# First stage of a transformer block on one Trainium2 core: two pairs of channels from the un-normalised input, one sum product, channels 2 and 3 in banks of their own

## Chip, cores and metric

One core of one Trainium2 chip (trn2) runs the whole program. The metric is device time in microseconds (us) of one execution. The kernel before took 2967.39 us as the median of 3 runs (2961.52, 2967.39 and 2967.43).

## The reference

The input x has 512 tokens of 1024 features. A first block adds attention and a gated linear recurrence to x, and then a layer of 128 x 128 experts; a second block adds a feed-forward layer, a mixer and a second feed-forward layer. The change touches only the recurrence at the very start of the first block:

```python
h = rms_norm(x, norm1_g)          # x * rsqrt(mean(x*x) + eps) * gain
z = h @ w_in
q, k, v, xr, yr, gate_logits = jnp.split(z, IN_SPLITS, axis=-1)
rnn = rg_lru(causal_depthwise_conv(xr, conv_w, conv_b), ...) * gelu(yr)
merged = gates[:, :, 0] * (attn @ w_br_attn) + gates[:, :, 1] * (rnn @ w_br_rnn)
```

xr and yr have 1280 columns each, ten blocks of 128, which the kernel calls channels c = 0 to 9. The root mean square of a token is a factor per token, so it may be put on x before the product with w_in or on the product after it. The convolution has four taps over the tokens. rg_lru takes two sigmoid gates from small products of the convolved channel (w_rg), forms a decay and an input, and scans over the tokens.

## The kernel before

Features lie on the 128 partitions and tokens along the free dimension, so X is 8 tiles (k = 0 to 7) of 128 x 512. Everything is computed in fp32 by a split: each operand is a high part (rounded to fp32r) and a low part (the rest), and a product of two 128-blocks is three matmuls, high x high, high x low and low x high (triple, L718 to L721). A weight unit of 128 output columns is 8 blocks, hence 24 matmuls of 512 columns (linear, L723). A weight unit is loaded by SP into one of 5 raw buffers (load, L2454), copied by ACT to its high part (split on ACT, L1281, recorded at L1279), and its low part is taken on DVE (split on DVE, L1760, recorded at L1750). Five pairs of high and low parts exist (NW = 5); the high part of unit j may be written when the product of unit j - 5 is done. The order of the units is written out by hand (unit_order). It begins with w_in 24, 34, 25, 35 (units 0 to 3: xr and yr of channels 0 and 1), then 26, 36, 27, 37 (units 4 to 7, channels 2 and 3), two units of gate columns (8, 9), two small w_rg units (10, 11), four units of channels 4 and 5 (12 to 15), and so on; the group of channels 8 and 9 has no gate columns, and the units after it are four of w_br_rnn (34 to 37, 640 columns) and two of w_rg (38, 39).

Each engine runs its own program in order, and they meet only at semaphores. The names that matter:

- SP: recurrence (L2481) issues the parameters, the four quarters of x, the constants cst, units 0 to 4, the lambdas and units 5 and 6. load waits before unit j until the low part of unit j - 5 is taken.
- ACT: recurrence (L1353) squares each tile of X into scr (L1276) and forms the high part of x times gain, gh (L1358). Then norm (L1305): the root from the sum (Ln and Exp in root, L1292) goes to scr[8], and eight high parts of the normalised H are copied. Then per channel d: the copy of the xr bank to pad (called xr_raw), the high part of the convolved channel (conv_hi), and the Gelu of the yr bank (gelu). Each change of function set on ACT is an ACT_TABLE_LOAD.
- DVE: gained (L1770) forms the low part of x times gain; norm (L1775) scales X into scr (L1758) and takes the low part of H (L1750). conv4 (L1815) is the convolution of one channel, four instructions and the low part of its result; for channel 0 it first scales xr and yr by the root. scalars (L1788) is a chain of some 35 tiny instructions for lambda and the softplus, with two Exp on ACT in it, and stands after channel 1. rnn_gates (L1832) is the DVE side of the gates and the scan.
- TensorE (PE): recurrence (L789) waits for cst, multiplies a matrix of ones with the 8 squares into bank 7 (sums, L754), then runs channel 0 from x times gain, the two units side by side (two, L733), so that it need not wait for the root. Channels 1 to 9 are products with the normalised H. After each pair from the second on: two gate units of the pair (gates_of_rnn, L762, called rgate) into banks 4 and 6, and the four small products of the pair before (rnn_products, L772, called br and bx) into banks 4 to 7.

PSUM has eight banks of 512 columns. xr of channel d goes to bank d % 2 and yr to bank 2 + d % 2, so channel d waits until channel d - 2 has been read. The product br of channel c waits for the sigmoid of the gate unit c (rgate) that read the same bank:

```python
q.wait_ge(dve, ("conv_parts", c))
if c < 6:
    q.wait_ge(act, ("rgate", c))
```

## Time and profile before

| | |
|---|---|
| median of 3 runs | 2967.39 us |
| the profiled execution | 2965.4 us |
| its span, first to last instruction | 2963.3 us |
| PE (matmul) busy | 2910.5 us, 98% |
| DVE, ACT, POOL busy | 64%, 39%, 28% |
| mean granted TensorE clock | 0.996 |

Times in rows are us from the start of the span. A row of a timeline is: start, duration, engine, line and operation, output<-inputs, shape and count, and in brackets the idle time of the engine before it and what ended it. Rows of matmuls overlap: a row's duration holds its way through the array, and the distance between two starts is what one costs in a stream. The 2.1 us between the span and the profiled execution's time lie outside the instructions. A granted clock of 1.00 is 2.4 GHz and 0.50 is 1.2 GHz.

### The profile page before, as it was taken

To read this page: it belongs to the slowest core of one execution; us is meant where nothing else is said; L and a number is where in the kernel's file an instruction comes from. 1 tells how busy PE (TensorE), PEld (TensorE's weight loads), DVE (VectorE), ACT (ScalarE), POOL (GpSimd) and SP (SyncE) were. 2 spreads that over 40 slices of the span, in tenths; PEclk is the share of its full clock that TensorE was granted. 3 is DMA by queue.
4 is the path that set the end of the run, shared out by engine and by line. 5 is a ranking of instruction groups with operands and counts; after the bars stand their busy time and mean duration, and the time that the engine had idled before them with its cause. 6 is when DMAs were issued, how large, how long until landed. Compare 5 with 4: busy or idle time off the path is not lost.

```text
span 2963.3 us, 35559 instructions
## 1 busy us (share of the span) xinstructions
PE 2910.5 (98%) x13947; PEld 2495.4 (84%) x13947; DVE 1909.2 (64%) x3257; ACT 1151.8 (39%) x1704; POOL 842.5 (28%) x521
## 2 busy tenths in 40 slices
PE   8999999999999999999999999999999999899999
PEld 6877777789889999998999999998888877688887
DVE  6664666578888895426878788865434577644443
ACT  5674565443333334433233223323222256632221
POOL 0000000128788888882332233321000300210000
PEclk9999999999999999999999999999999999999999
DMA  4325564436656676799988899842232321133222
GB/s 140 114 90 214 199 224 166 133 103 138 139 122 139 153 159 141 173 250 321 339 308 309 287 319 322 298 160 98 92 102 93 111 92 50 50 100 100 92 93 71
DMA packets 240807, 489.28 MB, mean 165 GB/s; under 512 B 97664, under 2 KB 149440, under 8 KB 240128
## 3 DMA queue, kind: packets, MB, share of 16 engines
q1 hardware_dynamic: 175680, 417.87, 43.0%
q0 software_dynamic: 64960, 69.14, 10.2%
q8 instruction: 110, 1.80, 0.2%
q14 instruction: 57, 0.47, 0.0%
HBM read 443.18 MB, written 77.23 MB: 176 GB/s over the span
## 4 chain that ended last, share of the span: by engine, by line
PE 80%; DVE 12%; ACT 4%; POOL 2%; issue 2%; DMA 1%; SPq 0%; POOLq 0%
PE pb L719 25%; PE pb L721 25%; PE pb L720 25%; DVE whl L1750 2%; POOL gd L2408 2%; ACT scr L1276 1%; DVE ST L1758 1%; DVE S L1750 1%; ACT whl L1279 1%; DVE su L1999 1%; DVE ST L2000 1%; DVE scr L1750 1%; DVE su L2002 1%; PE pb L1014 1%; DVE ST L1750 1%
## 5 line engine op out<-in xcount | busy, mean ns | idle before, releaser
L719 PE MATMUL pb<-H,whl 128*128 128x512 f32 (+1 forms) x2400 | 940.0, 392 | 6.4 <-DVE whl L1750 2.3
L721 PE MATMUL pb<-H,whl 128*128 128x512 f32 (+1 forms) x2400 | 911.8, 380 | 0.0
L720 PE MATMUL pb<-H,whl 128*128 128x512 f32 (+1 forms) x2400 | 911.2, 380 | 0.0
L1750 DVE TENSOR_TENSOR whl<-raw,whl 128x1024 fp32r<-128x1024 f32 (+5 forms) x554 | 652.5, 1192 | 252.7 <-ACT whl L1279 251.4
L1279 ACT ACTIVATE whl<-raw 128x1024 fp32r<-128x1024 f32 (+5 forms) x554 | 544.6, 1003 | 356.4 <-PE pb L721 355.2
L719 PE MATMUL pb<-S,whl 128*128 128x448 f32 (+2 forms) x1732 | 654.0, 378 | 13.9 <-DVE S L1750 6.1
L720 PE MATMUL pb<-S,whl 128*128 128x448 f32 (+2 forms) x1732 | 649.2, 375 | 0.0
L721 PE MATMUL pb<-S,whl 128*128 128x448 f32 (+2 forms) x1732 | 648.8, 375 | 0.0
L719 PEld LDWEIGHTS pb<-H,whl 128*128 128x128 f32 x2400 | 451.4, 188 | 84.0 <-issue 9.5
L720 PEld LDWEIGHTS pb<-H,whl 128*128 128x128 f32 x2400 | 451.4, 188 | 72.9 <-issue 6.0
L721 PEld LDWEIGHTS pb<-H,whl 128*128 128x128 f32 x2400 | 450.6, 188 | 72.3
L2408 POOL DMA_INDIRECT gd<-scr,place x256 | 438.5, 1713 | 137.7 <-issue 76.2
L719 PEld LDWEIGHTS pb<-S,whl 128*128 128x128 f32 x1732 | 327.0, 189 | 60.3 <-DVE S L1750 7.6
L720 PEld LDWEIGHTS pb<-S,whl 128*128 128x128 f32 x1732 | 327.2, 189 | 42.4 <-issue 1.0
L721 PEld LDWEIGHTS pb<-S,whl 128*128 128x128 f32 x1732 | 327.1, 189 | 42.4
L2387 POOL TENSOR_TENSOR pad<-X 128x512 f32<-128x512 f32 x31 | 43.5, 1404 | 856.5 <-DVE X L1750 828.8
L1276 ACT ACTIVATE scr<-pb 128x448 f32<-128x448 f32 (+1 forms) x130 | 70.9, 546 | 383.8 <-PE pb L721 359.8
L1750 DVE TENSOR_TENSOR scr<-pb,scr 128x512 f32<-128x512 f32 x96 | 66.0, 690 | 210.7 <-PE pb L721 199.7
L2441 POOL DMA_INDIRECT scr<-in_pv_rows,su x64 | 94.9, 1483 | 232.1 <-DVE scr L1758 204.8
L1279 ACT ACTIVATE S<-GA 128x896 fp32r<-128x896 f32 x60 | 57.2, 953 | 253.5 <-DVE GA L1750 253.5
L2395 POOL DMA_INDIRECT scr<-in_pu_rows,su x64 | 92.1, 1440 | 215.1 <-DVE scr L1758 166.4
L1750 DVE TENSOR_TENSOR X<-X,pb 128x448 f32<-128x448 f32 (+1 forms) x144 | 86.1, 628 | 91.0 <-PE pb L721 75.9
(226 smaller groups left out, 2516.7 us busy)
## 6 DMA issues: line engine op xcount, KB each, us to landing
raw<-in_pu SPq DMA_DIRECT2D x128, 512.0 KB, 4.4
raw<-in_pv SPq DMA_DIRECT2D x128, 512.0 KB, 6.2
raw<-in_w_in SPq DMA_DIRECT2D x72, 512.0 KB, 3.7
ad<-scr SPq DMA_DIRECT2D x128, 224.0 KB, 4.5
GA<-gd SPq DMA_DIRECT2D x60, 448.0 KB, 4.2
GA<-ad SPq DMA_DIRECT2D x60, 448.0 KB, 5.5
raw<-in_wg SPq DMA_DIRECT2D x44, 512.0 KB, 3.7
raw<-in_wu SPq DMA_DIRECT2D x44, 512.0 KB, 4.2
```

Source lines behind the costliest of these rows:

```text
L719: e.matmul(o, lh, h, start=start, stop=False, skip_group_check=True)
L720: e.matmul(o, lh, l, start=False, stop=False, skip_group_check=True)
L721: return e.matmul(o, ll, h, start=False, stop=stop, skip_group_check=True)
L1014: last = e.matmul(bank[gbank[n % 4]][:, c], hot2[n % 4][:, c], hot1[n % 4][:, c], start=True, stop=True, skip_group_check=True)
L1276: return e.activation(o, x, func, **kw)
L1279: return e.activation(o, x, ACT.Copy)
L1750: return e.tensor_tensor(o, x, y, op)
L1758: return e.scalar_tensor_tensor(out=o, in0=x, scalar=s, in1=y, op0=op0, op1=op1, **kw)
L2387: e.tensor_tensor(one_sq if k else sum_sq, x, x, ALU.mult).then_inc(pool.up(), 1)
L2395: e.indirect_dma_start(urow[j % 3] if j < UROWS else tail_row[j % 4], None, a["pu_rows"], bass.IndirectOffsetOnAxis(ap=expert[:, j:j + 1], ...
L2408: e.indirect_dma_start(g_rows, bass.IndirectOffsetOnAxis(ap=place[:, b, h, k:k + 1], axis=0), TSv[:, b, h, k:k + 1], None, compute_op=ALU. ...
L2441: e.indirect_dma_start(tail_row[j % 4], None, a["pv_rows"], bass.IndirectOffsetOnAxis(ap=expert[:, j:j + 1], axis=0)).then_inc(row_in[j % ...
```

## The change

TensorE. The 8 products for the sum of squares become one, of a tile scr[0] in which DVE has added the squares; it is issued after the first block (k = 0) of channel 1, and the wait for cst goes with it. Channels 0 and 1 both come from x times gain, by two. Channels 2 and 3 get banks 4 and 5 (xr) and 6 and 7 (yr) instead of 0 to 3. The banks 4 to 7 are those of the gate units and the small products, so the first of these now wait for the reads of channels 2 and 3 (xr_raw and gelu).

```diff
+        def x_bank(d):
+            return bank[(4 if d in (2, 3) else 0) + d % 2]
+        def y_bank(d):
+            return bank[(6 if d in (2, 3) else 2) + d % 2]
...
+        g1h, g1l = cut(S_t[:, 1024:5120], 8), cut(S_t[:, 6144:10240], 8)
...
-            def two(j, outs, hh, hl, ready, done, tag=None):
+            def two(j, outs, hh, hl, ready, done, tag=None, at_k=4):
...
-                    if k == 4 and tag:
+                    if k == at_k and tag:
...
             def sum_of(tag):
-                if tag == "4":
+                if tag == "1":
+                    q.wait_ge(cst_in, "cst")
+                    q.wait_ge(dve, "sq_sum")
+                elif tag == "4":
...
-                e.matmul(bank[7], ones, sum_sq, start=True, stop=True, skip_group_check=True).then_inc(
+                e.matmul(bank[7], ones, scr[0] if tag == "1" else sum_sq, start=True, stop=True, skip_group_check=True).then_inc(
...
-            def sums(tag, sq, b, lhs=ones):
-                for k, s in enumerate(sq):
-                    q.wait_ge(act, ("sq", tag, k))
-                    last = e.matmul(b, lhs, s, start=k == 0, stop=k == len(sq) - 1, skip_group_check=True)
-                last.then_inc(prod.up(("sums", tag)), 1)
...
             def gates_of_rnn(m):
...
-                q.wait_ge(act, ("r_sig", m - 2) if m > 1 else 0)
+                q.wait_ge(act, ("r_sig", m - 2) if m > 1 else ("gelu", 2) if m else ("xr_raw", 2))
...
             def rnn_products(pair):
...
+                    if c < 2:
+                        q.wait_ge(act, ("gelu", 3) if c else ("xr_raw", 3))
...
             def recurrence():
-                q.wait_ge(cst_in, "cst")
-                sums("1", scr[0:8], bank[7])
+                g1 = [("g", "1", k) for k in range(8)]
...
-                        if d == 0:
-                            j = q.unit("w_in", 24)
-                            q.unit("w_in", 34)
-                            two(j, (bank[0], bank[2]), gh, gl, [("g", "1", k) for k in range(8)], (("xr", 0), ("yr", 0)))
+                        if d < 2:
+                            j = q.unit("w_in", 24 + d)
+                            q.unit("w_in", 34 + d)
+                            two(j, (bank[i], bank[2 + i]), g1h, g1l, g1, (("xr", d), ("yr", d)), "1" if d else None, 1)
...
-                        if d == 2:
-                            q.wait_ge(dve, "xr_scaled")
-                        elif d > 2:
+                        if d in (4, 5):
+                            q.wait_ge(dve, ("xr_scaled", d - 4))
+                        elif d > 5:
...
-                        linear(q.unit("w_in", 24 + d), bank[i], Hh, Hl, h1, ("xr", d))
-                        if d > 1:
+                        linear(q.unit("w_in", 24 + d), x_bank(d), Hh, Hl, h1, ("xr", d))
+                        if d in (4, 5):
+                            q.wait_ge(dve, ("yr_scaled", d - 4))
+                        elif d > 5:
...
-                        linear(q.unit("w_in", 34 + d), bank[2 + i], Hh, Hl, h1, ("yr", d))
+                        linear(q.unit("w_in", 34 + d), y_bank(d), Hh, Hl, h1, ("yr", d))
...
```

ACT. A set of functions is loaded at the start, and the loads before the first Square and the first Ln are not asked for. The high parts of weights are mixed in among the squares, and in the loop over channels the high parts of up to three more units are made, at the head of each channel. Channel 1 has no copy to pad any more.

```diff
         def scalar(eng, e):
-            q, hi_done, logs = Waits(eng, units), [0], [False]
+            q, hi_done, logs = Waits(eng, units), [0], [True]
+            e.preload_act_table_set("natural_log_exp_and_others")
...
-            def norm(tag, sq, r, b, hi, mid=lambda: None, free=()):
+            def norm(tag, sq, r, b, hi, mid=lambda: None, free=(), between=lambda k: None):
...
+                    between(k)
...
             def recurrence():
...
-                for k in range(8):
-                    q.wait_ge(x_in[k // 2], ("x", k // 2))
-                    run(ACT.Square, scr[k], X[k]).then_inc(act.up(("sq", "1", k)), 1)
-                    e.activation(gh[k], X[k], ACT.Copy, scale=prm("norm1_g", k)).then_inc(act.up(("ghi", "1", k)), 1)
+                for k in range(10):
+                    if k < 8:
+                        q.wait_ge(x_in[k // 2], ("x", k // 2))
+                        e.activation(g1h[k], X[k], ACT.Copy, scale=prm("norm1_g", k)).then_inc(act.up(("ghi", "1", k)), 1)
+                    if k == 1:
+                        split(2)
+                    elif k > 1:
+                        run(ACT.Square, scr[k - 2], X[k - 2]).then_inc(act.up(("sq", "1", k - 2)), 1)
...
-                        split(2)
-                norm("1", scr, scr[8], bank[7], Hh, lambda: split(4))
+                        split(3)
+                    elif k == 7:
+                        split(4)
+                norm("1", scr, scr[8], bank[7], Hh, lambda: split(5), between=lambda k: split(6) if k == 5 else None)
...
-                        weights("w_in", 24 + d)
-                        if d == 0:
-                            weights("w_in", 34)
-                        if d:
+                        split(q.unit("w_in", 24 + d) + NW + 2)
+                        q.unit("w_in", 34 + d)
+                        if d > 1:
...
-                            q.wait_ge(dve, ("conv", d - 2) if d > 1 else ("pad0", i))
-                            copy(pad[i][:, 32:544], bank[i]).then_inc(act.up(("xr_raw", d)), 1)
+                            q.wait_ge(dve, ("conv", d - 2))
+                            copy(pad[i][:, 32:544], x_bank(d)).then_inc(act.up(("xr_raw", d)), 1)
...
-                        if d:
-                            weights("w_in", 34 + d)
...
-                        if d:
+                        if d > 1:
...
-                            q.wait_ge(dve, "yr_scaled")
-                        run(ACT.Gelu_apprx_tanh, rlf[d], bank[2 + i] if d else rlf[0]).then_inc(act.up(("gelu", d)), 1)
+                            q.wait_ge(dve, ("yr_scaled", d))
+                        run(ACT.Gelu_apprx_tanh, rlf[d], y_bank(d) if d > 1 else rlf[d]).then_inc(act.up(("gelu", d)), 1)
...
```

DVE. It adds the squares, takes low parts of weights inside norm, scales xr of channel 0 inside norm, and scales xr and yr of channel 1 as well as of channel 0 in conv4. In the loop the low parts of up to three more units are taken at the head of each channel.

```diff
-            def norm(tag, xs, gains, sq, r, hi, lo, mid=lambda: None):
+            def norm(tag, xs, gains, sq, r, hi, lo, mid=lambda: None, between=lambda k: None):
...
+                    between(k)
...
+            def scaled_x(c):
+                q.wait_ge(prod, ("xr", c))
+                tt(pad[c][:, 32:544], bank[c], scr[8], ALU.mult).then_inc(dve.up(("xr_scaled", c)), 1)
             def conv4(c, beside=()):
...
-                if c:
+                if c > 1:
...
-                    q.wait_ge(prod, ("xr", 0))
-                    then(tt(pad[0][:, 32:544], bank[0], scr[8], ALU.mult), "xr_scaled")
-                    q.wait_ge(prod, ("yr", 0))
-                    tt(rlf[0], bank[2], scr[8], ALU.mult).then_inc(dve.up("yr_scaled"), 1)
+                    if c:
+                        scaled_x(1)
+                    q.wait_ge(prod, ("yr", c))
+                    tt(rlf[c], bank[2 + c], scr[8], ALU.mult).then_inc(dve.up(("yr_scaled", c)), 1)
+                    q.wait_ge(dve, dve.n)
...
             def recurrence():
...
-                for k in range(8):
-                    gained("1", k, "norm1_g", gh, gl, ("g", "1", k))
-                    if k == 5:
+                for k in range(10):
+                    if k < 8:
+                        gained("1", k, "norm1_g", g1h, g1l, ("g", "1", k))
+                    if k == 1:
...
+                    elif k == 8:
+                        split(4)
+                    if k > 2:
+                        q.wait_ge(act, ("sq", "1", k - 2))
+                        then(tt(scr[0], scr[0], scr[k - 2], ALU.add), *(["sq_sum"] if k == 9 else []))
+                norm("1", X, gains("norm1_g"), scr, scr[8], Hh, Hl, between=lambda k: scaled_x(0) if k == 2 else split(5) if k == 4 else split(6) if k == 7 else None)
...
-                norm("1", X, gains("norm1_g"), scr, scr[8], Hh, Hl, lambda: split(4))
...
-                        weights("w_in", 24 + d)
-                        if d == 0:
-                            weights("w_in", 34)
+                        split(q.unit("w_in", 24 + d) + NW + 2)
+                        q.unit("w_in", 34 + d)
...
-                        if d:
-                            weights("w_in", 34 + d)
...
```

SP. Units 0 and 1 are loaded behind the first quarter of x, ahead of the other three.

```diff
-            def load_x(name):
-                for i in range(4):
+            def load_x(name, quarters=range(4)):
+                for i in quarters:
...
             def recurrence():
...
-                load_x("x")
+                load_x("x", (0,))
+                load(2)
+                load_x("x", (1, 2, 3))
...
+                q.wait_ge(dve, ("yr_scaled", 1))
...
```

The tiles g1h and g1l that hold x times gain are moved so that the results of channels 0 and 1 do not overwrite them.

## Rows read from the trace of the kernel before

**Rows 1.** The page: span, busy time of the engines

```profile
span 2963.3 us, 35559 instructions
...
PE 2910.5 (98%) x13947; PEld 2495.4 (84%) x13947; DVE 1909.2 (64%) x3257; ACT 1151.8 (39%) x1704; POOL 842.5 (28%) x521
```

**Rows 2.** Waits of PE, first 300 us: us in total, times, longest

```profile
PE pb L757 <- DMA cst<-in_cst: 11.5, 1, 11.5
PE pb L719 <- DVE whl L1750: 5.1, 3, 2.8
PE pb L719 <- ACT scr L1276: 1.6, 1, 1.6
```

**Rows 3.** Timeline of PE, 0 to 80 us

```profile
11.50 9.68 PE L757 MATMUL pb<-scr,cst 128*128 128x512 f32 x16 [11.50 <-DMA cst<-in_cst]
...
59.98 0.47 PE L719 MATMUL pb<-H,whl 128*128 128x512 f32 x1 [0.70 <-DVE whl L1750]
...
76.61 0.39 PE L719 MATMUL pb<-S,whl 128*128 128x512 f32 x1
...
79.33 0.39 PE L719 MATMUL pb<-H,whl 128*128 128x512 f32 x1
```

**Rows 4.** Timeline of DVE, 19 to 60 us

```profile
19.01 0.29 DVE L1754 TENSOR_SCALAR prm<-prm 128x1 f32<-128x1 f32 x3
...
19.72 2.32 DVE L1750 TENSOR_TENSOR whl<-raw,whl 128x1024 fp32r<-128x1024 f32 x2
23.89 1.42 DVE L1758 SCALAR_TENSOR_TENSOR scr<-X,prm,scr 128x512 f32<-128x512 f32 x2 [1.84 <-ACT scr L1276]
...
34.67 1.23 DVE L1750 TENSOR_TENSOR whl<-raw,whl 128x1024 fp32r<-128x1024 f32 x1 [0.25 <-ACT whl L1279]
35.81 0.68 DVE L1750 TENSOR_TENSOR pad<-pb,scr 128x512 f32<-128x512 f32 x1
...
43.63 1.23 DVE L1750 TENSOR_TENSOR whl<-raw,whl 128x1024 fp32r<-128x1024 f32 x1 [2.20 <-ACT whl L1279]
...
49.32 1.22 DVE L1750 TENSOR_TENSOR whl<-raw,whl 128x1024 fp32r<-128x1024 f32 x1 [0.26 <-ACT whl L1279]
50.46 0.35 DVE L1750 TENSOR_TENSOR sm<-scr 128x64 f32<-128x64 f32 x2
...
59.75 0.54 DVE L1755 TENSOR_SCALAR ST<-pad,prm 128x512 f32<-128x512 f32 x1
```

**Rows 5.** Timeline of ACT, 0 to 113 us

```profile
5.95 1.28 ACT L1276 ACT_TABLE_LOAD   x1 [5.95 <-DMA X<-in_x]
...
40.72 1.28 ACT L1276 ACT_TABLE_LOAD   x1
42.02 0.63 ACT L1276 ACTIVATE ST<-ST 128x512 f32<-128x512 f32 x1
...
55.55 1.05 ACT L1279 ACTIVATE whl<-raw 128x1024 fp32r<-128x1024 f32 x1
...
72.85 0.69 ACT L1276 ACTIVATE scr<-pb,prm 128x512 f32<-128x512 f32 x1
...
112.17 0.69 ACT L1276 ACTIVATE scr<-pb,prm 128x512 f32<-128x512 f32 x1 [1.00 <-PE pb L721]
```

**Rows 6.** Timeline of the weight loads of PE, 11 to 17 us

```profile
15.93 0.34 PEld L757 LDWEIGHTS pb<-scr,cst 128*128 128x128 f32 x1 [0.52 <-issue]
16.73 0.19 PEld L757 LDWEIGHTS pb<-scr,cst 128*128 128x128 f32 x1 [0.46 <-issue]
```

**Rows 7.** Timeline of PE, 168 to 202 us

```profile
177.54 0.76 PE L719 MATMUL pb<-S,whl 128*128 128x512 f32 x1 [2.84 <-DVE whl L1750]
...
195.77 0.50 PE L719 MATMUL pb<-S,whl 128*128 128x512 f32 x1 [1.60 <-DVE whl L1750]
...
199.05 0.50 PE L719 MATMUL pb<-H,whl 128*128 128x512 f32 x1 [1.61 <-ACT scr L1276]
```

**Rows 8.** PE by windows of 1 us: window, busy, granted clock, DMA share, GB/s

```profile
178.00:179.00 1.00, 1.00 (x4) 0.50 0.42 122
```

## The prediction

> **What bounds the kernel now.** I read the page first: PE is busy 2910.5 of 2963.3 us [rows 1]. Only work taken from PE or its idle time can pay, and PE idles 52.8 us in all. The waits of PE over the first 300 us come next [rows 2]: 11.5 us for cst at the start, then 5.1 us for low parts of weights and 1.6 us for an ACT result. The timeline of PE places them [rows 3]: it starts at 11.50 with sixteen matmuls of the eight sum products, which take 9.68 us, and from there to 174 us it pauses once, for 0.70 us. So in this stage PE looks like the bound. The timelines of DVE and ACT must be read beside it [rows 4, 5], because the first stage is also one long chain through both: root, H, convolutions, the tiny `scalars`, Gelu, gates. Its slack behind PE is small: at 112.17 ACT waited 1.00 us for PE [rows 5], and that is all there is in a cycle of 35 us. The chain even overtakes PE at the end of the stage, where PE idles 2.84, 1.60 and 1.61 us [rows 7].
>
> What can be won is easy to count. The chain decides whether it is kept. A few terms recur: a matmul in a stream costs (79.33 - 76.61) / 12 = 0.227 us [rows 3], a unit of 24 costs 5.44, one block of one unit 0.68; a high part takes ACT 1.0 and its low part DVE 1.15 to 1.2 [rows 4, 5].
>
> **The start.** The first quarter of x has landed at 5.95 [rows 5] and cst at 11.50 [rows 3], four transfers later: 1.4 us for each. Units 0 and 1, now second and third in the queue, land at about 7.3 and 8.7, and the other quarters of x some 2.8 us later than before. The table load of 1.28 us at 5.95 moves into the time in which nothing has landed. High part, low part: PE starts at about 9.6 instead of 11.50. The clock is low at first: the weight loads of PE shrink from 0.34 to 0.19 us between 15.93 and 16.73 [rows 6], so 5.2 us ran at half speed. I take the same 5.2 us now, a loss of 2.6. Channel 0 then ends at 9.6 + 16 x 0.68 + 2.6 = 23.1, block 0 of channel 1 at 24.5, and the one sum product (0.9; 1.2 is the mean of the eight [rows 3], which includes slow ones) at 25.4. Is the sum of squares there by then? From the first high part at about 7.3 on DVE has 8 low parts of x (0.75), 4 of weights (1.2) and 7 adds (0.7, as the product of 35.81): 15.7 us, so 23.0 [rows 4]. Just in time; two more microseconds of waits for ACT would move the root by 0.6.
>
> Ln and Exp then take 1.4, with no table load between: DVE begins to scale X at 26.8. Before, it began at 23.89 [rows 4]. **The root comes 2.9 us later**, although 7 of 8 products are gone, since channel 0 now stands ahead of it. Bounds: 1.5 us to either side, by the clock and the landings.
>
> A table load in the rows costs 1.30 us: at 40.72 it begins, at 42.02 the Gelu runs [rows 5]. The Trainium skill (ScalarE: Activation LUTs, What ACT_TABLE_LOAD costs) adds a drain of about 1.38 us, 2.66 in all; by that the removed load before Ln would give back 1.4 us more, and my sum would read +3.5 instead of +4.9. The trace shows no such gap, so it decides.
>
> **What DVE does between root and channel 2.** Before, from 23.89 to the convolution of channel 2 at 59.75 [rows 4], 35.9 us. The change adds, from the same rows: low parts of units 8 and 9 (2.3) and of the small unit 10 (0.45), now at the head of channels 1 and 2; scaling of xr and yr of channel 1 (2 x 0.68); the small prm and mask instructions that stood before the root (19.01 to 19.72, 0.7). It saves 0.4: waits for high parts of 0.25, 2.20 and 0.26 us become one of 2.3 (the Gelu of channel 0 with its table load, then a high part). That is +4.4. **The convolution of channel 2 starts at 26.8 + 40.3 = 67.1, 7.3 us later than before.** `scalars`, at 50.46 before, starts at 57.3.
>
> **Where PE is meanwhile.** After the sum product: seven blocks of two units 9.5, four units 21.8, and 0.9 of waiting for the last H tiles (ready at 26.8 + 10.5 + 2.95, the three inserts in norm). It has finished channels 2 and 3, by their four banks without a wait, at 57.6. Before it was there at 59.98 + 5.5 = 65.5. **PE is 8 us ahead.** But the next is gate unit 0 in bank 4, which now waits for xr_raw of channel 2. On ACT that copy stands behind the two Exp of `scalars`, Gelu of channel 1 and high parts 9 and 10. Before, a high part stood 5.1 us after the start of `scalars` (50.46 to 55.55 [rows 4, 5]); now that point is 62.4 and the copy is done at 64.2. PE waits 6.6 us. Its two gate units take 10.9 us and some 1.7 to 3.4 more at a low clock: done at 77 to 78.5.
>
> Behind them br of channel 0 waits for the sigmoid of rgate 0, which ACT issues after channels 2 and 3: at 72.85 before [rows 5]. It inherits +7.3 from the convolution, less one high part of 1.0 and 0.3 of another that have moved ahead: 78.9, done at 79.6. br ran at 76.61 before [rows 3]. **All 8 us are spent and PE is 3.0 us late.** SP is no limit: units 5 and 6 are asked for behind the same low parts, and its new wait for yr_scaled 1 comes long after.
>
> **Channels 4 to 7.** PE was the bound and had slack 1.0 us of ACT behind it [rows 5]. The high and low parts at the head of a channel delay rgate by another 0.75 us relative to PE; under 1.0, so nothing is added and +3.0 is carried.
>
> **The end of the stage.** The units of w_br_rnn are now ready early, so the wait of 2.84 us at 177.54 goes. What is late next is the low part of unit 39 and the sigmoid of channel 8, which stand behind the gates of channels 6 and 7. For them, parts at the head of channels 8 and 9 add about 2.5 us and three of 640 columns that no longer stand later save about 2.0: +0.5. So PE waits once, some 6 us, instead of three times, and goes on at 199.05 + 3.5.
>
> **The clock.** After the 2.84 us of idle PE ran at 0.50 [rows 7, 8] for about 3 us; after 1.60 us it did not. The 6 us wait at the end costs a like stretch: 1.7 us, half of it hidden, so 0.9. The 2.0 us wait before br lies between the two rows: 0 or 1.7; I take 0.5. The rest of the program is bound by PE and shifts whole.
>
> **Sum:** 3.0 + 0.5 + 0.9 + 0.5 = +4.9 us on the profiled 2965.4, so 2970.3. That execution lies 2.0 below the median of the runs shown, 2967.39, which gives 2972. A measurement of this kernel can tell about 0.2%, 5.9 us, from no change.
>
> **The rivals.**
> Faster: the chain keeps up, or my order of it is wrong, and PE keeps its lead. For it: PE idles almost nowhere before. Against it: ACT's slack of 1.00 us and the 7.3 us counted on DVE. It needs xr_raw 2 by 57.6, 6.6 us before my estimate. Time: 2967.4 - 8.0 = 2959.4. Chance 0.12. Something halfway, 0.05.
> Slower: the clock. If the wait before br lowers it (1.7), and the long wait at the end holds it low for two such stretches, none hidden (3.4), the sum is 3.0 + 0.5 + 1.7 + 3.4 = +8.6: 2976. [...] The Trainium skill (TensorE: Matmul & The Clock Gate, Part 1) speaks for it: low is the resting state of the clock and activity lifts it. The trace agrees (0.34 then 0.19 us at the start). Chance 0.20.
> The change doesn't do what it says: the early table load doesn't hold for Ln, or units 0 and 1 land together with x. The root comes another 1.3 to 2 us late, and the sum is 6.2 to 6.9: 2974. Chance 0.08.
> My forecast has 0.55, of which 0.12 lies above the 5.9 us.
>
> **Numbers.** Faster 0.12; within 0.2%: 0.43 + 0.05 + 0.04 = 0.52; slower 0.12 + 0.20 + 0.04 = 0.36. Range: the bounds of the root (1.5), of the chain (1) and of the clock (0 to 3.4) span about +1.5 to +10; downwards it also takes in the halfway case and a run as low as the lowest shown. 2962 to 2979.
>
> **What would show it.** PE starts near 9.6; one sum product near 25; DVE scales X from 26 to 27; convolution of channel 2 near 67; PE idle 6 to 7 us for an ACT copy to pad near 64, and 2 us before the first small product at 79 to 80; no wait at 175; one of 5 to 7 us near 199, at a clock of 0.50 behind it. I am wrong if PE passes 58 to 64 us without a wait, or if the first small product starts before 76.6.

## The result and the profile after

The changed kernel takes 2972.56 us in the median of 10 runs (2967.37 to 2977.41), the kernel before 2967.23 us (10 runs, 2961.52 to 2970.21). The ratio is 1.0020, with a 95% interval of 1.0011 to 1.0029: slower by 5.3 us on the medians, just under the 5.9 us that the prediction called no change, and clear of zero. The profiled execution took 2973.16 us with a span of 2971.4. A second series of the unchanged file gave 2968.64 us (11 runs) beside 2964.47 (28 runs), ratio 1.0013 (1.0004 to 1.0022). One profile of the experiments, that of banks_undone, fell on a disturbed execution (mean clock 0.753) and is not read; the median below is of its other 11 runs.

The page and the waits of PE over the first 300 us of the kernel after:

```profile
span 2971.4 us, 35561 instructions
...
PE 2909.3 (98%) x13933; PEld 2495.9 (84%) x13933; DVE 1913.4 (64%) x3266; ACT 1150.6 (39%) x1702; POOL 842.6 (28%) x521
```

```profile
PE pb L726 <- DVE whl L1762: 15.4, 3, 9.0
PE pb L726 <- ACT pad L1287: 6.5, 1, 6.5
PE pb L726 <- ACT scr L1284: 1.9, 2, 1.6
PE pb L726 <- DVE H L1762: 0.5, 1, 0.5
```

Beside [rows 1, 2]: the first wait has shrunk from 11.5 to 9.0 us, and 6.5 us stand at a new place, a wait for ACT's copy to pad. All waits together were 18.2 us and are now 24.3. The timeline of PE, over the same stretches as [rows 3, 7]:

```profile
9.02 0.77 PE L726 MATMUL pb<-S,whl 128*128 128x512 f32 x1 [9.02 <-DVE whl L1762]
...
23.88 1.02 PE L761 MATMUL pb<-scr,cst 128*128 128x512 f32 x2
...
39.05 0.50 PE L726 MATMUL pb<-H,whl 128*128 128x512 f32 x1 [0.51 <-DVE H L1762]
...
63.57 0.80 PE L726 MATMUL pb<-H,whl 128*128 128x512 f32 x1 [6.46 <-ACT pad L1287]
...
78.86 0.47 PE L726 MATMUL pb<-S,whl 128*128 128x512 f32 x1 [1.57 <-ACT scr L1284]
...
81.70 0.39 PE L726 MATMUL pb<-H,whl 128*128 128x512 f32 x1
...
198.65 0.80 PE L726 MATMUL pb<-S,whl 128*128 128x512 f32 x1 [5.90 <-DVE whl L1762]
...
201.92 0.57 PE L726 MATMUL pb<-H,whl 128*128 128x512 f32 x1 [0.34 <-ACT scr L1284]
```

PE is through with channels 2 and 3 at 63.57 - 6.46 = 57.1, where it was at 65.5 before: 8.4 us ahead. It then gives all of that back. The first small product comes at 78.86 against 76.61, gate unit 6 at the end of the stage at 201.92 against 199.05. DVE and ACT, over the stretches of [rows 4, 5]:

```profile
26.39 1.42 DVE L1770 SCALAR_TENSOR_TENSOR scr<-X,prm,scr 128x512 f32<-128x512 f32 x2 [3.70 <-ACT scr L1284]
...
48.74 2.36 DVE L1762 TENSOR_TENSOR whl<-raw,whl 128x1024 fp32r<-128x1024 f32 x2 [2.20 <-ACT whl L1287]
...
56.55 0.35 DVE L1762 TENSOR_TENSOR sm<-scr 128x64 f32<-128x64 f32 x2
...
66.18 0.54 DVE L1767 TENSOR_SCALAR ST<-pad,prm 128x512 f32<-128x512 f32 x1
```

```profile
0.74 1.28 ACT L1271 ACT_TABLE_LOAD   x1 [0.74 <-PEq L2802]
...
24.94 0.69 ACT L1284 ACTIVATE scr<-pb,cst 128x512 f32<-128x512 f32 x1 [4.21 <-PE pb L761]
...
45.18 0.63 ACT L1287 ACTIVATE S<-ST 128x512 fp32r<-128x512 f32 x1 [5.18 <-DVE ST L1770]
45.83 1.28 ACT L1284 ACT_TABLE_LOAD   x1
47.12 0.63 ACT L1284 ACTIVATE ST<-ST 128x512 f32<-128x512 f32 x1
...
62.94 0.58 ACT L1287 ACTIVATE pad<-pb 128x512 f32<-128x512 f32 x1
...
78.03 1.27 ACT L1284 ACTIVATE scr<-pb,prm 128x512 f32<-128x512 f32 x2
...
114.55 0.69 ACT L1284 ACTIVATE scr<-pb,prm 128x512 f32<-128x512 f32 x1 [1.35 <-PE pb L728]
```

The convolution of channel 2 starts at 66.18 instead of 59.75, and the sigmoid of rgate 0 at 78.03 instead of 72.85. The small product starts 0.83 us behind the start of that sigmoid now; before, it came 3.76 us behind, so the chain had 2.9 us to spare there.

**A mark behind the stage.** Single executions of one kernel spread over 8 us and more, so the stage is also judged by one row behind it, an early copy of the attention for which ACT has waited 7.72 us on PE in every profile that is read here. These are its rows in the kernel before and after:

```profile
256.54 0.60 ACT L1279 ACTIVATE ST<-pb 128x512 f32<-128x512 f32 x1 [7.72 <-PE pb L721]
```

```profile
259.44 0.60 ACT L1287 ACTIVATE ST<-pb 128x512 f32<-128x512 f32 x1 [7.72 <-PE pb L728]
```

In the second profiles of both kernels it stands at 256.87 and 259.82. The stage costs 2.9 to 3.0 us, twice. The rest of the 8.1 us by which the two first spans differ came later, behind the stage that the change is about: the second profile of the changed kernel has a span of 2964.8, with the stage as long as in the first.

### The profile page after: what moved, and what is told of

The parts are those of the page before. It is cut to its first block, busy times and chain, and to the rows that moved or that the text cites. A ratio compares the mean times of both kernels' runs of the same rounds, so it can differ in the third digit from the quotient of the medians.

```text
span 2971.4 us, 35561 instructions
## 1 busy us (share of the span) xinstructions
PE 2909.3 (98%) x13933; PEld 2495.9 (84%) x13933; DVE 1913.4 (64%) x3266; ACT 1150.6 (39%) x1702; POOL 842.6 (28%) x521
## 4 chain that ended last, share of the span: by engine, by line
PE 80%; DVE 13%; ACT 4%; issue 2%; POOL 1%; DMA 1%; SPq 0%; ACTq 0%; POOLq 0%; DVEq 0%
PE pb L726 25%; PE pb L728 25%; PE pb L727 25%; DVE whl L1762 3%; ACT scr L1284 2%; DVE ST L1770 1%; PE pb L1021 1%; DVE ST L1762 1%; DVE S L1762 1%; ACT whl L1287 1%; DVE su L2020 1%; DVE ST L2021 1%; DVE su L2023 1%; DVE scr L1762 1%; POOL gd L2429 1%
## 5 line engine op out<-in xcount | busy, mean ns | idle before, releaser
L726 PE MATMUL pb<-S,whl 128*128 128x448 f32 (+2 forms) x1748 | 661.7, 379 | 28.1 <-DVE whl L1762 15.4
L727 PE MATMUL pb<-S,whl 128*128 128x448 f32 (+2 forms) x1748 | 656.3, 375 | 0.0
L728 PE MATMUL pb<-S,whl 128*128 128x448 f32 (+2 forms) x1748 | 656.2, 375 | 0.0
L726 PEld LDWEIGHTS pb<-S,whl 128*128 128x128 f32 x1748 | 330.6, 189 | 75.8 <-issue 14.2
L728 PEld LDWEIGHTS pb<-S,whl 128*128 128x128 f32 x1748 | 330.7, 189 | 43.5
L727 PEld LDWEIGHTS pb<-S,whl 128*128 128x128 f32 x1748 | 331.0, 189 | 42.9 <-issue 1.0
```

What stands on the lines that cost most here:

```text
L726: e.matmul(o, lh, h, start=start, stop=False, skip_group_check=True)
L727: e.matmul(o, lh, l, start=False, stop=False, skip_group_check=True)
L728: return e.matmul(o, ll, h, start=False, stop=stop, skip_group_check=True)
```

## The experiments

The edits are against the changed kernel, except for the last one. The small product is the first br, the mark is the row above. Ln is the first step of the root on ACT, and "from Ln" is the time from its start to the small product: it leaves out how early or late the root of that execution was. The first rows are the profiles of the two kernels.

| kernel | Ln, us | small product, us | from Ln, us | mark, us | median, us | before beside it | ratio, 95% |
|---|---|---|---|---|---|---|---|
| kernel before | 22.50 | 76.61 | 54.11 | 256.54 | 2967.23 | | |
| before_again | 22.85 | 76.98 | 54.13 | 256.87 | 2963.47 (one run) | 2964.37 | |
| changed kernel | 24.94 | 78.86 | 53.92 | 259.44 | 2972.56 | 2967.23 | 1.0011 to 1.0029 |
| after_again | 25.39 | 79.34 | 53.95 | 259.82 | 2968.64 | 2964.47 | 1.0004 to 1.0022 |
| fill_before_root | 31.45 | 85.39 | 53.94 | 267.53 | 2975.12 | 2964.47 | 1.0025 to 1.0049 |
| fill_after_root | 23.86 | 77.80 | 53.94 | 261.09 | 2970.22 | 2964.47 | 1.0010 to 1.0028 |
| banks_undone | not read | not read | not read | not read | 2969.53 | 2964.47 | 1.0000 to 1.0018 |
| scalars_after_channel_3 | 24.37 | 76.34 | 51.97 | 260.38 | 2968.11 | 2964.37 | 1.0001 to 1.0020 |
| scalars_early | 25.54 | 72.16 | 46.62 | 255.60 | 2962.26 | 2964.37 | 0.9979 to 0.9997 |
| scalars_early_banks_undone | 25.52 | 75.83 | 50.31 | 256.56 | 2965.91 | 2964.37 | 0.9994 to 1.0012 |
| sum_before_channel_1 | 23.61 | 77.53 | 53.92 | 258.03 | 2970.88 (one run) | 2965.03 | |
| tail_as_before | 25.61 | 79.53 | 53.92 | 261.58 | 2969.87 | 2965.03 | 1.0003 to 1.0022 |
| early_sum_tail | 24.87 | 71.49 | 46.62 | 251.51 | 2959.34 | 2965.03 | 0.9973 to 0.9991 |
| before_scalars_early | 23.47 | 75.66 | 52.19 | 255.56 | 2961.99 | 2965.03 | 0.9985 to 1.0003 |

The chain theory is that of the prediction: root, convolutions, `scalars`, Gelu and gates on DVE and ACT decide when the small products run. The main rival has PE as the bound, with the loss coming from somewhere else. Two plain repeats came with these.

The column "from Ln" speaks for the chain by itself. In the six profiles that leave the chain as the change made it (the changed kernel twice, the two fills, sum_before_channel_1 and tail_as_before) the small product comes 53.92 to 53.95 us behind Ln, although Ln moves between 23.61 and 31.45 and the wait of PE for the copy to pad between 1.36 and 6.46 us. In the kernel before it is PE that comes last. Rows of ACT with the table load and Ln in the kernel before, then Ln in fill_before_root and in fill_after_root:

```profile
21.20 1.28 ACT L1269 ACT_TABLE_LOAD   x1 [1.00 <-PE pb L757]
22.50 0.69 ACT L1276 ACTIVATE scr<-pb,cst 128x512 f32<-128x512 f32 x1
```

```profile
31.45 0.69 ACT L1286 ACTIVATE scr<-pb,cst 128x512 f32<-128x512 f32 x1 [10.57 <-PE pb L763]
```

```profile
23.86 0.69 ACT L1287 ACTIVATE scr<-pb,cst 128x512 f32<-128x512 f32 x1 [3.33 <-PE pb L761]
```

> The changed kernel as it is, for a second profile and an interval on the same chip. Chain theory: PE waits 6.5 us for the copy to pad near 57 to 63.6 us and the first small product starts at 78.9 again, 2.3 us later than in the kernel before; time 3 to 6 us over the kernel before. Rival (the 5 us of the medians are clock phases alone): the stage ends as early as before and only the number of stretches at a clock of 0.50 differs.

> The kernel before as it is, for a second profile. Either theory: first small product at 76.6 us, PE waits of 2.8, 1.6 and 1.6 us between 174 and 199 us; what differs from its first profile after 210 us is the spread of one execution to the next.

The repeat of the changed kernel waits 6.42 us before its gate unit, and its small product comes at 79.34; the repeat of the kernel before has it at 76.98. Its three waits at the end of the stage were 2.85, 1.40 and 1.62 us. The loss is in the stage and not in the clock alone.

### The same work on PE before and behind the root

```diff
 # fill_before_root, in sum_of, behind the wait for cst
+for _ in range(7):
+    e.matmul(bank[6], ones, X[0], start=True, stop=True, skip_group_check=True)
 q.wait_ge(dve, "sq_sum")
```

```diff
 # fill_after_root, behind the products of channel 1
+if d:
+    for _ in range(7):
+        e.matmul(bank[6], ones, X[0], start=True, stop=True, skip_group_check=True)
 continue
```

> Seven more products of ones with X[0] (6.0 us of PE) ahead of the one sum product, so ahead of the root. Chain theory: the root, all of the convolutions and the first small product come 6 us later (84.9 us), the wait for the copy to pad stays near 6.5 us, and the time grows by about 6 us to 2978. Rival (the lead of PE is idle anyway, so PE work costs nothing in this stage): the wait shrinks by 6 us and the time stays.

> The same seven products (6.0 us of PE) behind channel 1, so behind the root's sum. Chain theory: they fill the wait of 6.5 us for the copy to pad, which shrinks to about 0.5 us; the first small product stays at 78.9 us and the time changes by less than 1 us (2972), perhaps 0.5 less as the clock stays up. Rival (PE is the bound of the stage): every later product comes 6 us later and the time is 2978.

Timelines of PE, first fill_before_root, then fill_after_root:

```profile
70.08 0.79 PE L726 MATMUL pb<-H,whl 128*128 128x512 f32 x1 [6.44 <-ACT pad L1289]
...
85.39 0.47 PE L726 MATMUL pb<-S,whl 128*128 128x512 f32 x1 [2.68 <-ACT scr L1286]
```

```profile
62.50 0.50 PE L726 MATMUL pb<-H,whl 128*128 128x512 f32 x1 [1.36 <-ACT pad L1290]
...
77.80 0.77 PE L726 MATMUL pb<-S,whl 128*128 128x512 f32 x1 [2.84 <-ACT scr L1287]
```

Ahead of the root, 6 us of work push the small product from 79 to 85.4 and cost 6.5 us against after_again (2975.12 to 2968.64), and the wait of 6.4 us stays whole. (Against after_again the small product is 6.0 us later and the mark 7.7: behind a wait of 2.68 us in front of the small product the granted clock fell to 0.50 here too.) Behind the root the same work fills the wait, which falls to 1.36 us, and the small product is no later; that it is 1.1 us earlier than at 78.86 comes from this execution's root (its first convolution starts at 41.16 and not at 42.24). This parts the two theories: only what stands ahead of the root is paid for. The 1.6 us by which fill_after_root still exceeds after_again was not expected, and it has a place; as the root of this execution was early, it hides a larger loss: from the small product to gate unit 6 (203.61) this profile takes 2.75 us more than the changed kernel. Its gate units now run at full clock, so PE is done sooner and waits 2.84 us in front of the small product. Behind that wait the clock is down (windows of 2 us: busy, PEld, DVE, ACT and POOL busy, granted clock, DMA share, GB/s):

```profile
78.00:80.00 2.00, 2.00 (x5) 1.59 (x6) 0.79 (x1) 1.72 (x3) 0.00 (x0) 0.50 0.82 172
80.00:82.00 2.00, 2.00 (x6) 1.54 (x5) 0.98 (x2) 1.41 (x4) 0.00 (x0) 0.50 0.85 316
```

In windows of 1 us the clock is at 0.50 from 77 to 83 us. From here on PE is the bound, so the slow stretch shows. In the changed kernel it lay behind the long wait at 63.57, where the gate units had time to spare.

### The four banks

```diff
 # banks_undone (and the same on scalars_early)
-return bank[(4 if d in (2, 3) else 0) + d % 2]
+return bank[d % 2]
-return bank[(6 if d in (2, 3) else 2) + d % 2]
+return bank[2 + d % 2]
...
-q.wait_ge(act, ("r_sig", m - 2) if m > 1 else ("gelu", 2) if m else ("xr_raw", 2))
+q.wait_ge(act, ("r_sig", m - 2) if m > 1 else 0)
...
-if c < 2:
-    q.wait_ge(act, ("gelu", 3) if c else ("xr_raw", 3))
...
+if d in (2, 3):
+    q.wait_ge(dve, ("xr_scaled", d - 2))
...
+if d in (2, 3):
+    q.wait_ge(dve, ("yr_scaled", d - 2))
```

> Channels 2 and 3 back in banks 0 to 3. Chain theory: PE now waits near 45 to 52 us for xr of channel 1 to be scaled instead of near 57 to 63.6 us, the first small product stays at 78.9 us and the time stays within 1 us: the four banks bought nothing here. Rival (the added waits of the gate units and small products on the four banks cause the loss): the first small product returns to 76.6 us or earlier and the time falls by 2 us or more.

> The same with channels 2 and 3 back in banks 0 to 3. Chain theory: now that the chain is short, PE binds, and it waits near 45 to 52 us for the scaled xr of channel 1; first small product near 73.5 instead of 70.9: the four banks are worth 2.6 us; time 2967. Rival (the banks never matter): the same time as with the banks.

In the changed kernel, banks or no banks cannot be told apart: 2969.53 beside 2968.64, the intervals overlap nearly whole. The rival, 2 us or more less, is not borne out by the time; where PE waited in this kernel no profile shows. With the chain shortened (the next experiment) they differ: 2965.91 against 2962.26. The timeline of PE in scalars_early_banks_undone has the waits for the scaled xr and yr where they were expected, and the small product 3.7 us later than with the banks (75.83 against 72.16; 2.6 was expected, which did not count that the clock is at 0.50 from 53 to 56 us behind the wait of 3.74):

```profile
42.84 0.51 PE L726 MATMUL pb<-H,whl 128*128 128x512 f32 x1 [1.46 <-DVE ST L1760]
...
52.33 0.50 PE L726 MATMUL pb<-H,whl 128*128 128x512 f32 x1 [3.74 <-DVE pad L1760]
...
75.83 0.39 PE L726 MATMUL pb<-S,whl 128*128 128x512 f32 x1
```

The mark shows only 1.0 us of it (256.56 against 255.60). The rest is the clock in scalars_early: PE waits 2.16 us in front of the small product there and behind it the clock is at 0.50 from about 73.5 to 76.5 us, where the other kernel does not wait at all (1.7 us, from the small product to gate unit 6), and the low clock at the end of the stage costs it 1.0 us more.

### The chain of tiny instructions

```diff
 # scalars_after_channel_3, on DVE and for the two Exp on ACT
-if d == 1:
+if d == 3:
```

```diff
 # scalars_early, DVE: scalars up to neglam, with minus_abs ahead of the wait for
 # lambda_exps, goes ahead of norm; the rest is softplus()
+scalars()
 norm("1", X, gains("norm1_g"), scr, scr[8], Hh, Hl, between=...)
...
-if d == 1:
-    scalars()
+if d == 3:
+    softplus()
 # ACT: the two Exp go ahead of norm
+split(5)
+q.wait_ge(dve, "lambda_sums")
+run(ACT.Exp, sm_t[:, 2:4], sm_t[:, 0:2]).then_inc(act.up("lambda_exps"), 1)
+q.wait_ge(dve, "minus_abs")
+run(ACT.Exp, sq[1], sq[1]).then_inc(act.up("softplus_exp"), 1)
-norm("1", scr, scr[8], bank[7], Hh, lambda: split(5), between=...)
+norm("1", scr, scr[8], bank[7], Hh, between=...)
```

> The changed kernel with the chain of tiny instructions (scalars) and its two Exp behind channel 3 instead of channel 1. Chain theory: the wait of PE for the copy to pad shrinks from 6.5 to about 1.2 us and the convolution of channel 2 starts near 58.3 instead of 66.2; but the Exp pair and its table loads still stand ahead of rgate 0, so the first small product comes only 2.7 us earlier (76.2), behind a wait of some 7 us; time 2970. Rival (scalars is not what holds the chain): no change at 78.9.

> The changed kernel with the first part of scalars and its two Exp ahead of the root, where DVE idles 3.7 and ACT 4.2 us and the set for Exp is loaded anyway, and the rest (softplus, 5 us of DVE) behind channel 3. Chain theory: root unchanged at 26.4; convolution of channel 2 near 58.4 (66.2 now); first small product near 70.9, 8 us earlier than now and 5.7 earlier than in the kernel before; two table loads less; time 2964, 3 to 5 us under the kernel before. Rival (PE or the banks bind): the small product stays near 76 to 79 and the time near 2970.

Timelines of PE, first scalars_after_channel_3, then scalars_early:

```profile
57.64 0.50 PE L726 MATMUL pb<-H,whl 128*128 128x512 f32 x1 [1.09 <-ACT pad L1287]
...
76.34 0.77 PE L726 MATMUL pb<-S,whl 128*128 128x512 f32 x1 [7.49 <-DVE sm L1766]
```

```profile
58.81 0.50 PE L726 MATMUL pb<-H,whl 128*128 128x512 f32 x1 [1.09 <-ACT pad L1287]
...
72.16 0.47 PE L726 MATMUL pb<-S,whl 128*128 128x512 f32 x1 [2.16 <-DVE sm L1766]
...
193.52 0.79 PE L726 MATMUL pb<-S,whl 128*128 128x512 f32 x1 [5.87 <-DVE whl L1762]
...
196.79 0.79 PE L726 MATMUL pb<-H,whl 128*128 128x512 f32 x1 [0.35 <-ACT scr L1284]
```

Moved behind channel 3, `scalars` gives back the wait at the gate unit (6.46 to 1.09 us) and puts nearly all of it in front of the small product (1.57 to 7.49), as the two Exp with their table loads still stand ahead of rgate 0; the small product gains 2.5 us, 0.6 of it by the earlier root of this execution. (The bracket names a tiny instruction of DVE, but the sigmoid of rgate 0 starts at 75.51, again 0.83 us ahead of the small product.) The mark gains nothing (260.38): the 7.49 us of idle lower the clock where PE is the bound, and so do the 5.9 us at the end of the stage.

Taken apart, `scalars` costs the chain next to nothing. Its sums and the Exp run while DVE waits for the root and the set for Exp is loaded; this is ACT in scalars_early:

```profile
23.68 0.49 ACT L1284 ACTIVATE sm<-sm 128x2 f32<-128x2 f32 x2 [2.78 <-DVE sm L1808]
25.54 0.69 ACT L1284 ACTIVATE scr<-pb,cst 128x512 f32<-128x512 f32 x1 [1.37 <-PE pb L761]
```

The small product comes 6.7 us earlier than in the changed kernel (8.0 expected; the root of this execution was 0.6 later, and DVE waits 0.78 us, until 58.01, for a high part that stands on ACT behind the Gelu of channel 1). From Ln it is 46.62 us where it was 53.9. The median is 2962.26, 2.1 us under the kernel before beside it, with an interval that excludes 1, where that of the changed kernel lies above 1: the chain is what held the small products. `scalars` itself stands in both kernels. What the change added to the chain is the later root and the work listed in the prediction; taking the first part of `scalars` out gives back more than that.

### The root and the end of the stage

```diff
 # sum_before_channel_1
-two(j, (bank[i], bank[2 + i]), g1h, g1l, g1, (("xr", d), ("yr", d)), "1" if d else None, 1)
+two(j, (bank[i], bank[2 + i]), g1h, g1l, g1, (("xr", d), ("yr", d)), "1" if d else None, 0)
```

```diff
 # tail_as_before, ACT (DVE alike)
-split(q.unit("w_in", 24 + d) + NW + 2)
-q.unit("w_in", 34 + d)
+if d < 8:
+    split(q.unit("w_in", 24 + d) + NW + 2)
+    q.unit("w_in", 34 + d)
+else:
+    weights("w_in", 24 + d)
...
 copy(cvh[d % 4], rhf[d]).then_inc(act.up(("conv_hi", d)), 1)
+if d > 7:
+    weights("w_in", 34 + d)
```

> The one sum product directly behind channel 0 (the sum of squares is there 0.1 us earlier). Chain theory: root 1.35 us earlier (25.1), the wait for the copy to pad shrinks by nothing, since that copy and PE's next products both move, but the first small product moves to 77.5 and gate unit 6 to 200.6; time 1.3 us less. Rival (the root is not on the path): no product after 70 us moves.

> The changed kernel with the weight parts at the head of channels 8 and 9 where they stood in the kernel before. Chain theory: PE waits three times again (2.9, 1.6 and 1.6 us) instead of once for 5.9, gate unit 6 starts 0.6 us earlier (near 201.3 instead of 201.9), and no stretch of 6.8 us at a clock of 0.50 follows the long wait; time 0.5 to 2 us less than the changed kernel, 2967. Rival (the early low parts help at the end of the stage): gate unit 6 starts 2 us or more later.

Timelines of PE, first sum_before_channel_1, then tail_as_before:

```profile
22.47 1.10 PE L761 MATMUL pb<-scr,cst 128*128 128x512 f32 x2 [0.57 <-DVE scr L1762]
...
77.53 0.47 PE L726 MATMUL pb<-S,whl 128*128 128x512 f32 x1 [1.68 <-ACT scr L1284]
...
200.53 0.53 PE L726 MATMUL pb<-H,whl 128*128 128x512 f32 x1 [0.35 <-ACT scr L1284]
```

```profile
180.57 0.47 PE L726 MATMUL pb<-S,whl 128*128 128x512 f32 x1 [2.84 <-DVE whl L1767]
...
198.80 0.50 PE L726 MATMUL pb<-S,whl 128*128 128x512 f32 x1 [3.01 <-DVE whl L1767]
...
202.07 0.80 PE L726 MATMUL pb<-H,whl 128*128 128x512 f32 x1 [1.01 <-ACT scr L1284]
```

Against the first profile of the changed kernel the sum product is 1.4 us earlier, and so are the small product, gate unit 6 and the mark (1.3 to 1.4 us each). One to one, over 180 us: the root is on the path. How much of the 1.4 us the edit itself brought is less sure: PE started 0.16 us earlier in this execution and ran at half speed for 4.0 us instead of 5.3, and the sum product then waited 0.57 us for the adds. The whole execution (2970.88) shows nothing of it, which says how little one time tells here.

tail_as_before: gate unit 6 at 202.07 looks like no gain, but the root of this execution stood 0.7 us later than in the first profile (Ln at 25.61 against 24.94). Against its own root it is 0.5 us earlier, as expected. What failed is the clock. The first wait of 2.84 us did not lower it this time, so PE reached the second wait sooner; that became 3.01 us and not 1.6 and lowered it instead, just where PE is the bound. Gate unit 6 starts slow (0.80 us), and from it to the mark it takes 59.5 us, 2.0 more than in the changed kernel. The time missed the 0.5 to 2 us that were expected: alone, this edit bought nothing.

### A version that beats both

early_sum_tail joins scalars_early, sum_before_channel_1 and tail_as_before.

> All three together: first part of scalars ahead of the root, sum product directly behind channel 0, end of the stage as in the kernel before. Chain theory: first small product 1.3 us earlier than with scalars early alone (70.9 against 72.2), gate unit 6 near 195 against 199.05 in the kernel before, no long stretch at a clock of 0.50 at the end of the stage; time 2960 to 2961, 3.5 to 4.5 us under the kernel before. Rival (another bound stands behind the chain): no more than with scalars early alone, 2962.

```profile
58.14 0.50 PE L726 MATMUL pb<-H,whl 128*128 128x512 f32 x1 [0.62 <-ACT pad L1287]
...
71.49 0.47 PE L726 MATMUL pb<-S,whl 128*128 128x512 f32 x1 [2.17 <-DVE sm L1771]
...
194.01 0.50 PE L726 MATMUL pb<-H,whl 128*128 128x512 f32 x1 [1.61 <-ACT scr L1284]
```

2959.34 us beside 2965.03, ratio 0.9982 (0.9973 to 0.9991). From Ln to the small product it is 46.62 us, as in scalars_early. Gate unit 6 stands 5.0 us before that of [rows 7] and the mark 5.0 us before its own, so that the clock took nothing. The sum product had to wait 1.56 us for the adds of DVE in this execution, and the small product gained 0.7 us instead of 1.3.

Last, the same cure without the disease, on the kernel before:

```diff
 # before_scalars_early, on the kernel before, DVE (the two Exp on ACT go ahead of norm as above)
-norm("1", X, gains("norm1_g"), scr, scr[8], Hh, Hl, lambda: split(4))
+split(4)
+scalars()
+norm("1", X, gains("norm1_g"), scr, scr[8], Hh, Hl)
...
-if d == 1:
-    scalars()
+if d == 3:
+    softplus()
```

> The kernel before with only the first part of scalars ahead of the root and the rest behind channel 3. Chain theory: there PE was the bound up to 174 us and the chain had slack, so only the wait of 0.70 us near 60 us goes: first small product at 75.9 instead of 76.6, time 0.7 us less, no difference that runs can tell. Rival (scalars costs 8 us wherever it stands): 5 us or more less.

The small product comes at 75.66 (0.95 us earlier), the mark 1.0 us earlier; the runs can't tell it from no change (0.9985 to 1.0003). There PE had no lead, so a shorter chain buys it only the wait of 0.70 us in [rows 3]; the other 0.25 us is this execution's earlier start (PE at 11.25 instead of 11.50). Its root came 1.0 us later than in the kernel before, and the small product was not later for it. The changed kernel bought the lead and not the chain. At the mark the chain alone is worth 1.0 us, the change alone loses 2.9, and early_sum_tail, which has both and two smaller edits, gains 5.0. The runs alone part early_sum_tail from the kernel before, but not clearly from before_scalars_early: the two intervals overlap.

## Why the prediction was right

The time (2972.56 for 2972.0) and the case forecast are right, and so is the mechanism, wait by wait. That the time fits to 0.6 us is luck: the terms of the stage were too large, and something outside the stage made up for it.

- **The start.** PE at 9.02 (9.6 forecast), sum product at 23.88 (24.5), DVE at 26.39 (26.8): root 2.5 us late, not 2.9. The landings came a little sooner. The matmuls stand 0.43 us apart until 14.29, so half speed lasted 5.3 us for the 5.2 taken over. That this fits is luck: the same start ran at half speed until 12.14 in fill_after_root and until 15.37 in scalars_early, which moves the root by as much as 1.7 us from one execution to the next. The step holds, and sum_before_channel_1 shows that the root counts in full.
- **Root to channel 2 on DVE.** 39.8 us against 40.3; before, 35.9. Channel 2 at 66.18 for 67.1, `scalars` at 56.55 for 57.3. Each added item is there, and the wait of 2.20 us is the one that had been named.
- **The lead of PE.** Done with channel 3 at 57.1 for 57.6, a wait of 6.46 us for 6.6, on the copy to pad. fill_after_root shows the lead to be idle time.
- **The small product.** 78.86 for 79.6, behind a wait of 1.57 for 2.0. Over [rows 3] it is 2.25 us late, where the sum had 3.0; this term was 0.75 too large, the errors of the steps above it added up. By the rows, Ln is 2.44 us late, the way from Ln to the sigmoid of rgate 0 is 2.74 us longer (53.09 for 50.35), and 2.93 us of that the chain had to spare: 2.25.
- **Channels 4 to 7.** At 114.55 ACT waits 1.35 us for PE and a cycle later 0.78, where it was 1.00 each time before: PE is the bound and the lateness is carried, as forecast.
- **The end of the stage.** The wait near 175 is gone, one wait of 5.90 us has taken its place, and gate unit 6 is 2.87 us late, 0.6 more than the small product for +0.5 forecast.
- **The clock.** A 0.50 stretch follows both long waits, as forecast. The 1.7 us of a stretch is what windows of 1 us give for the one before (granted clock 0.54, 0.50, 0.50 and 0.76 from 177 to 181, 1.7 us short of full speed); what it cost PE was 1.4, as from the first wait to the second PE takes 16.6 us there and 15.2 in tail_as_before, where the clock stayed up. The 0.9 and 0.5 us put down for it were a mean over something with two outcomes. In the two profiles of the changed kernel it costs next to nothing (the mark is 2.9 us late, gate unit 6 was 2.9); in scalars_early and scalars_after_channel_3 the same wait at the end costs 1.3 and 1.1 us, because there the low clock outlasted the start of gate unit 6. In front of the small product the wait of 1.57 us lowered nothing, so the 0.5 was 0. Of the slower rival the mechanism is real and the 3.4 us are too much.
- **The sum.** +4.9 was forecast for the stage and +2.9 is what the mark shows. The medians say +5.3 and +4.2. Of the two intervals (3.3 to 8.6 and 1.2 to 6.5 us) the second holds 2.9 and the first just misses it. Whether the difference behind the stage is chance or an effect of the shift on clock and transfers is open; two profiles of the same changed kernel differ there by 7 us, half of it idle time of PE (34.6 against 31.1 us in windows of 10 us).
- **The table load.** The changed kernel has one load less between the sum product and the root. From the end of the sum products to the first scaling on DVE it was 23.89 - 21.18 = 2.71 us before and is 26.39 - 24.90 = 1.49 now: 1.22 us less, about the 1.28 of the load. The load at 45.83 starts 0.02 us behind the activation before it (45.18 + 0.63), and the Gelu follows 0.01 us behind its end. The Trainium skill (ScalarE: Activation LUTs, What ACT_TABLE_LOAD costs) puts a drain of about 1.38 us on top, and this trace does not agree: an estimate by that figure had the root at 25.4, and it came at 26.39.

## What to carry to other kernels

An engine that is 98% busy and idles nowhere in a stage may still have a chain of the other engines at its heels. Before work is taken from it, ask how much later that chain may be, and look for what is on it that could stand elsewhere: here a lead of 8 us met a chain with 3 us to spare that the change had made 5 us later. With the tiny instructions in the middle of it moved into a wait for the root the small product came 6.7 us sooner and the kernel was 2 us faster than the one before (1 us at the mark), and with two more edits 5 us. To tell who binds, put the same dummy work once ahead of and once behind the suspected point. And judge an edit of 3 us in 3000 by a row just behind the stage, since whole executions spread more than that, and take off how late the root of that execution was: from Ln to the small product six profiles agree within 0.03 us.

## What was not expected of the hardware

- A wait of PE can cost twice. After 2.84 us of idle in front of the small product of fill_after_root the granted clock was 0.50 from 77 to 83 us, and the work that followed was on the path. The same low clock after the 6.46 us wait of the changed kernel cost nothing, since PE had to wait again behind it.
- Which wait lowers the clock can't be told from its length alone. After waits of 1.57 us and, in early_sum_tail, 2.17 us in front of the small products it was not lowered; after 2.16 us in scalars_early it was. After 2.84 us it was lowered in the kernel before, and in tail_as_before, behind a wait of the same 2.84 us (180.57), it was not.
- In tail_as_before the clock fell between 199 and 200 us, behind the wait of 3.01 us that had ended at 198.80 and ahead of the one of 1.01, and stood at 0.50 until 206.
- The start differs from one execution of the same work to the next: PE begins at 8.9 to 9.4 us in all profiles of the changed kernel and its variants, but it runs at half speed for 3.1 us in fill_after_root, 5.3 in the changed kernel and 6.3 in scalars_early, and the root follows (Ln at 23.86, 24.94 and 25.54).
